# First mixer: scores from a stacked 128-row product and one of 64 rows, merge factors from one product of 48 rows

## What is computed

```python
for g, (win, dil) in enumerate(DILATED_GROUPS):
    o, lse = dilated_band_attention(q[:, :, g], k[:, :, g], v[:, :, g], win, dil)
    # inside: s = einsum('nbqhd,nbphd->nhbqp', q_blocks, key_band) / sqrt(64); softmax; times v
y = merge_by_denominator(outs, lses)      # softmax over the 3 groups' lse, weighted sum
y = y @ w_o
```

## Time and profile before

| | us |
|---|---|
| median of 3 runs | 3315.78 (3310.75 to 3321.85) |
| the profiled execution's own time | 3310.81 |
| its span in the profile | 3309.0 |
| PE busy | 3141.3 (95%) |
| PE weight loads busy | 3039.6 (92%) |
| VectorE, ScalarE, GpSimd busy | 1784.8, 1620.8, 1700.9 |
| mean granted TensorE clock | 0.974 of full |

### The profile page before, as it was taken

The page is one execution under the profiler, slowest core; times in us unless marked ns, Lnnn a source line. Parts: engine busy times, 40 slices in busy tenths (PEclk is TensorE's granted clock), DMA queues, the critical chain, the costliest instruction groups (busy, mean ns, idle before and its releaser), DMA issues. The chain is left out here.

```text
span 3309.0 us, 56628 instructions
## 1 busy us (share of the span) xinstructions
PE 3141.3 (95%) x21560; PEld 3039.6 (92%) x21560; DVE 1784.8 (54%) x3643; ACT 1620.8 (49%) x3402; POOL 1700.9 (51%) x1420
## 2 busy tenths in 40 slices
PE   8999999999999968999999999689889999999997
PEld 7999999999999948999999999688878999999997
DVE  4445445454554537765463465348867653533653
ACT  4555555555555514454353354247745543543542
POOL 5555555555555505665465465343336654554663
PEclk9999999999999979999999999799989999999998
DMA  5666666676667275333444444211153344444443
GB/s 202 244 241 218 231 234 224 215 258 217 234 229 257 87 273 188 128 134 126 139 137 134 147 137 147 90 48 40 46 176 120 130 135 134 156 136 141 162 144 98
DMA packets 134861, 540.74 MB, mean 163 GB/s; under 512 B 25008, under 2 KB 49376, under 8 KB 131760
## 3 DMA queue, kind: packets, MB, share of 16 engines
q1 hardware_dynamic: 133392, 535.79, 47.8%
q10 hardware_dynamic: 784, 1.12, 0.1%
q0 software_dynamic: 416, 0.21, 0.0%
HBM read 497.34 MB, written 216.90 MB: 216 GB/s over the span
## 5 line engine op out<-in xcount | busy, mean ns | idle before, releaser
L1236 ACT CAST t_w_hi<-t_raw 128x1024 fp32r<-128x1024 f32 (+1 forms) x456 | 468.2, 1027 | 796.0 <-PE t_bank L103 732.0
L101 PE MATMUL t_bank<-x_hi,t_w_hi 128*128 128x352 f32 (+1 forms) x2112 | 680.9, 322 | 6.0 <-DVE x_lo L1530 2.7
L102 PE MATMUL t_bank<-x_lo,t_w_hi 128*128 128x352 f32 (+1 forms) x2112 | 675.1, 320 | 0.0
L1359 POOL TENSOR_TENSOR t_w_lo<-t_raw,t_w_hi 128x1024 fp32r<-128x1024 f32 (+1 forms) x228 | 544.4, 2388 | 253.1 <-ACT t_w_hi L1236 253.1
L103 PE MATMUL t_bank<-x_hi,t_w_lo 128*128 128x352 f32 (+1 forms) x2112 | 671.9, 318 | 0.0
L1437 DVE TENSOR_TENSOR t_w_lo<-t_raw,t_w_hi 128x1024 fp32r<-128x1024 f32 (+1 forms) x228 | 326.7, 1433 | 639.9 <-ACT t_w_hi L1236 639.9
L101 PE MATMUL a_gemm<-x_hi,a_w_hi 128*128 128x352 f32 (+1 forms) x1728 | 564.0, 326 | 11.3 <-DVE x_lo L620 11.3
L102 PE MATMUL a_gemm<-x_lo,a_w_hi 128*128 128x352 f32 (+1 forms) x1728 | 553.8, 321 | 0.0
L103 PE MATMUL a_gemm<-x_hi,a_w_lo 128*128 128x352 f32 (+1 forms) x1728 | 551.8, 319 | 0.0
L101 PE MATMUL t_bank<-t_h_hi,t_w_hi 128*128 128x352 f32 (+1 forms) x1440 | 466.6, 324 | 33.0 <-DVE t_h_lo L1443 24.9
L103 PE MATMUL t_bank<-t_h_hi,t_w_lo 128*128 128x352 f32 (+1 forms) x1440 | 463.3, 322 | 0.0
(11 more groups left out here) (280 smaller groups left out, 5799.6 us busy)
## 6 DMA issues: line engine op xcount, KB each, us to landing
t_raw<-w_up SPq DMA_DIRECT2D x264, 512.0 KB, 3.7
roll<-cache SPq DMA_DIRECT2D x128, 1023.5 KB
t_raw<-w_down SPq DMA_DIRECT2D x96, 512.0 KB, 3.6
a_raw<-w_a SPq DMA_DIRECT2D x72, 512.0 KB, 4.5
roll<-cache SPq DMA_DIRECT2D x16, 2044.0 KB
t_raw<-w_o SPq DMA_DIRECT2D x48, 512.0 KB, 3.6
t_raw<-w_down SPq DMA_DIRECT2D x48, 384.0 KB, 3.1
vT<-a_vt SPq DMA_DIRECT2D x24, 516.0 KB, 6.7
```

Of the source, the lines that this page charges most:

```text
L101: pe.matmul(out, w_hi, x_hi, start=first, stop=False)
L102: pe.matmul(out, w_hi, x_lo, start=False, stop=False)
L1236: act.copy(w_hi[:, b % RING, cols], raw[:, b % RING, cols]).then_inc(s_whi, 1)
L1359: pool.tensor_tensor(w_lo[:, b % RING, cols], raw[:, b % RING, cols], f32(w_hi[:, b % RING, cols]), ALU.subtract).then_inc(s_wlo[0], 1)
```

## The change

Three edits, all in `mixer_a`:

- **Scores.** The keys' high part and low part of a head stand under one another in one tile `k_both` (own 64 partitions: high; the other 64: low), and the queries' high part stands twice (`q_twice`). One matmul of 128 rows makes q_hi·k_hi + q_hi·k_lo; one of 64 rows adds q_lo·k_hi. Per query block the order is: 128 rows head 0, 128 rows head 1, 64 rows head 0, 64 rows head 1.
- **The parts' making.** ACT writes the high part in two copies of 64 partitions (one a head), and for queries in two more to the other half; POOL subtracts in two instructions of 64 partitions. POOL's next turn also waits until its own last subtraction is done, and from `s_qtwo` that the copies of the queries have read `qp`; PE's `scores` at s = 0 wait for `s_qtwo` too.
- **Factors.** High and low factors stand in one tile `f_both` of 48 rows (0 to 15 and 32 to 47, zeros between), and `sel` holds its matrix twice, so that one matmul of 48 rows takes the place of two of 16. The merge weighs in place, and two additions take the place of the reduction.

```diff
@@ scalar: high_turned
-                act.copy(class_tiles(kq_hi[i1 % 2][:, r // 3, :], g1)[:, :, a:b],
-                         class_major(qp[:, r % 2, 0:n], g1)).then_inc(s_kqhi, 1)
+                dst = (k_both, q_twice)[r // 3][i1 % 2]
+                for h in range(2):
+                    last = act.copy(class_tiles(dst[own_half(h), h, :], g1)[:, :, a:b],
+                                    class_major(qp[own_half(h), r % 2, 0:n], g1))
+                last.then_inc(s_kqhi, 1)
+                if r >= 3:
+                    for h in range(2):
+                        last = act.copy(class_tiles(dst[other_half(h), h, :], g1)[:, :, a:b],
+                                        class_major(qp[own_half(h), r % 2, 0:n], g1))
+                    last.then_inc(s_qtwo, 1)
@@ gpsimd: turn
+                need(pool, s_qtwo, 3 * i1 + (-1, 0, 0, 0, 0, 1)[r])
...
-                pool.tensor_tensor(lo, class_major(qp[:, r % 2, 0:n], g1), f32(hi), ALU.subtract).then_inc(s_kqlo, 1)
+                hi_of = (k_both, q_twice)[r // 3][i1 % 2]
+                for h in range(2):
+                    lo = k_both[i1 % 2][other_half(h), h, :] if r < 3 else q_lo[i1 % 2][own_half(h), :]
+                    last = pool.tensor_tensor(class_tiles(lo, g1)[:, :, a:b],
+                                              class_major(qp[own_half(h), r % 2, 0:n], g1),
+                                              f32(class_tiles(hi_of[own_half(h), h, :], g1)[:, :, a:b]), ALU.subtract)
+                last.then_inc(s_kqlo, 1)
+                need(pool, s_kqlo, k + 1)
@@ vector: merge_tile
-                dve.tensor_reduce(o[:, p % 2, 0, j * P:(j + 1) * P], fbm[:, :, :].rearrange("p g t -> p t g"),
-                                  op=ALU.add, axis=AX_X).then_inc(s_fbr, 1)
+                dve.tensor_tensor(weighed[:, 0, :], weighed[:, 0, :], weighed[:, 1, :], ALU.add).then_inc(s_fadd, 1)
+                need(dve, s_fadd, k + 1)
+                dve.tensor_tensor(weighed[:, 0, :], weighed[:, 0, :], weighed[:, 2, :], ALU.add).then_inc(s_fbr, 1)
@@ tensor: spread_factors and scores
-                pe.matmul(x_bank[:, 0:NG * P], sel[:, j, :], rhs[0], start=True, stop=False)
-                pe.matmul(x_bank[:, 0:NG * P], sel[:, j, :], rhs[1], start=False, stop=True).then_inc(s_fb, 1)
+                pe.matmul(x_bank[:, 0:NG * P], sel[:, j, :], f_both[:, :, :].rearrange("r g t -> r (g t)"), start=True,
+                          stop=True).then_inc(s_fb, 1)
...
                     for h in range(2):
-                        rows = slice(HD * h, HD * h + HD)
...
-                        product(pe, s_bank[h][:, 2 * P * j + w0:2 * P * (j + 1)],
-                                kq_hi[i % 2][rows, 1, q_cols], kq_lo[i % 2][rows, 1, q_cols],
-                                kq_hi[i % 2][rows, 0, k_cols], kq_lo[i % 2][rows, 0, k_cols],
-                                True, True).then_inc(s_scores, 1)
+                        pe.matmul(out[h], q_twice[i % 2][:, h, q_cols], k_both[i % 2][:, h, k_cols], start=True, stop=False)
+                    for h in range(2):
+                        rows = own_half(h)
+                        pe.matmul(out[h], q_lo[i % 2][rows, q_cols], k_both[i % 2][rows, h, k_cols], start=False,
+                                  stop=True).then_inc(s_scores, 1)
```

More of the change, by code:

```diff
@@ L191, in mixer_a, with small_rows @@
         o = sb("o", [P, 2, NG, T])
-        fbm = sb("fbm", [P, NG, P])
         st = sb("st", [P, 2, 96])
         stT = sb("stT", [96, P])
[L195 to L199, removed]
-        qs, ks = (sb(name, [P, NG, PAIRS, NS]) for name in ("qs", "ks"))
[L201 to L205, removed]
+        qs, ks = (sb(name, [P, NG, PAIRS, NS]) for name in ("qs", "ks"))
+        with ExitStack() as upper:
+            f_both, sel = (upper.enter_context(nc.sbuf_tensor("a_" + name, shape, F32R)) for name, shape in (
+                ("f_both", [48, NG, P]), ("sel", [48, QT, P])))
+        f_hi, f_lo = f_both[0:16], f_both[32:48]
+        below = sb("below", [P, (2 * NG + QT) * P])
+        def small_rows(first, n, shape):
+            return below[64:80, first * P:(first + n) * P].rearrange(shape, g=NG, t=P)
+        sr = small_rows(0, 2 * NG, "r (w g t) -> r w g t")
+        dd, mw = (small_rows(k * NG, NG, "r (g t) -> r g t") for k in (2, 3))
+        mt = below[64:80, 4 * NG * P:(4 * NG + 1) * P]
+        fw = below[0:16, (NG + QT) * P:(2 * NG + QT) * P].rearrange("r (g t) -> r g t", g=NG)
+        q_lo = [sb(f"q_lo{i}", [P, SEQ], F32R) for i in range(2)]
+        k_both, q_twice = [None, sb("k_both1", [P, 2, SEQ], F32R)], [None, sb("q_twice1", [P, 2, SEQ], F32R)]
         with ExitStack() as lent:
@@ L213, in mixer_a @@
             w_lo = sb_lent("w_lo", [P, 2, KT, P])
-            kq_hi[0] = sb_lent("kq_hi0", [P, 2, SEQ])
-            kq_lo[0] = sb_lent("kq_lo0", [P, 2, SEQ])
+            k_both[0] = sb_lent("k_both0", [P, 2, SEQ])
+            q_twice[0] = sb_lent("q_twice0", [P, 2, SEQ])
         units_kv = sb("units_kv", [P, 8, KT, P])
@@ L227, in mixer_a @@
         s_whi, s_wlo, s_gemm, s_evac = (sem(x) for x in ("whi", "wlo", "gemm", "evac"))
-        s_shuf, s_t1, s_t2, s_qp, s_kqhi, s_kqlo = (sem(x) for x in ("shuf", "t1", "t2", "qp", "kqhi", "kqlo"))
+        s_shuf, s_t1, s_t2, s_qp, s_kqhi, s_kqlo, s_qtwo, s_fadd = (
+            sem(x) for x in ("shuf", "t1", "t2", "qp", "kqhi", "kqlo", "qtwo", "fadd"))
         kq_out = [sem("kq_out0"), sem("kq_out1")]
@@ L292, in stats_due, with own_half, other_half @@
             return q if 0 <= i < NI and q > 0 and g == 0 and s == 2 else None
+        def own_half(h):
+            return slice(HD * h, HD * h + HD)
+        def other_half(h):
+            return own_half(1 - h)
         def first_key(u, j):
@@ L498, in evacuate @@
                     if i1 == 0:
-                        act.wait_ge(s_sel, 1)
+                        act.wait_ge(s_sel, 2)
                 need(act, s_gemm, 9 * i1 + c + 1)
@@ L622, in _ @@
             dve.wait_ge(s_const, 16 * 6)
-            dve.tensor_copy(sel[:, :, :].rearrange("r j f -> r (j f)"), vt[0:16, 0:QT * P]).then_inc(s_sel, 1)
+            dve.tensor_copy(f_both[0:32, :, :].rearrange("r g t -> r (g t)"), vt[0:32, 0:NG * P]).then_inc(s_sel, 1)
+            dve.wait_ge(s_sel, 1)
+            dve.tensor_copy(sel[:, :, :].rearrange("r j f -> r (j f)"), vt[0:48, 0:QT * P]).then_inc(s_sel, 1)
             def natural(ap3, g):
@@ L833, in scores @@
                     need(pe, s_kqlo, 6 * (i + 1))
+                    need(pe, s_qtwo, 3 * (i + 1))
                 if u == 0:
@@ L838, in scores @@
                     t, w0 = 2 * s + j, first_key(u, j)
+                    q_cols, k_cols = slice(t * P, (t + 1) * P), slice((t - 1) * P + w0, (t + 1) * P)
+                    out = [s_bank[h][:, 2 * P * j + w0:2 * P * (j + 1)] for h in range(2)]
                     for h in range(2):
-                        rows = slice(HD * h, HD * h + HD)
-                        q_cols, k_cols = slice(t * P, (t + 1) * P), slice((t - 1) * P + w0, (t + 1) * P)
-                        product(pe, s_bank[h][:, 2 * P * j + w0:2 * P * (j + 1)],
-                                kq_hi[i % 2][rows, 1, q_cols], kq_lo[i % 2][rows, 1, q_cols],
-                                kq_hi[i % 2][rows, 0, k_cols], kq_lo[i % 2][rows, 0, k_cols],
-                                True, True).then_inc(s_scores, 1)
+                        pe.matmul(out[h], q_twice[i % 2][:, h, q_cols], k_both[i % 2][:, h, k_cols], start=True, stop=False)
[3 more added lines that the diff above has]
+                                  stop=True).then_inc(s_scores, 1)
             def weigh_values(u):
@@ L2370, in shape_constants @@
         mask_c=np.where((q <= i) & (q // HD == i // HD), f(0), big).astype(f))
-    sel = np.zeros((2 * QT, QT, P), f)
+    sel = np.zeros((48, QT, P), f)
     for r in range(2 * QT):
-        sel[r, r % QT, HD * (r // QT):HD * (r // QT) + HD] = 1
-    out["sel"] = sel.reshape(2 * QT, QT * P)
+        for part in (0, 32):
+            sel[part + r, r % QT, HD * (r // QT):HD * (r // QT) + HD] = 1
+    out["sel"] = sel.reshape(48, QT * P)
     row = np.arange(P)
```

10 lines of the change are left out of this document (4 added, 6 removed).

## The result

| us | before | after |
|---|---|---|
| median (4 runs each) | 3313.27 (3308.93 to 3321.85) | 3465.43 (3461.82 to 3469.63) |
| the profiled execution's own time | 3310.81 | 3461.82 |
| mean granted TensorE clock | 0.974 | 0.960 |

The changed kernel takes 1.0456 times as long (95% interval 1.0432 to 1.0480). I had predicted 3400 us and a range of 3330 to 3432: the direction is right, the size is not, and the time lies outside the range.

The account below looks back on a forecast made before the run. PE was taken to bound the loop, busy 1081.9 of 1083.0 us. Own time 3310.8 + 24.7 (PE's own sum) + 64.8 (waits for POOL) = 3400.3 us; forecast 3400 us, range 3330 to 3432.

Parts of the forecast that it names:

- Slots on PE: Scores on PE: three slots a block as before, 64-row pairs sharing one, narrow 128-row products at 0.115 us; no time saved.
- Changes of height: PE switching between matmuls of different row counts: 0.14 us (narrow) or 0.19 us (wide) each, 31.3 + 4.5 us in all.
- The spread: Factors' spread on PE: the low part's product goes, 0.18 us x 56 = -10.1 us in the loop.
- POOL's and ACT's chain: Making of key and query parts: each POOL turn +1.9 us from ACT's two copies and POOL's two subtractions.
- PE's waits for the scores: PE waiting for POOL: 8 x 4.5 us (group 1) + 8 x 3.1 us (group 2) + some 4 us (first set).
- ACT's evacuations of chunks 6 to 8: Projection chunks on PE waiting for ACT's evacuations, held back by turn 4's copies: counted at nothing.
- The wait in group 0: PE before group 0's scores: POOL done at 619.1 against PE at 620.0, so no wait, but only just.
- rival C: Sixteen PE waits of some 4 us lower the clock, losing 2 us more each: 3432 us; chance 0.10.
- my own walk: Group-1 set followed turn by turn on the earlier trace's clock: POOL done at 670.8, PE ready at 666.3, waiting 4.5 us.
- Rival A: Only the changes between row counts on PE cost; POOL's halves are cheap or slack suffices: 3336 us; chance 0.15.
- B: Not slower: the gaps read as row-count changes on PE belong to semaphore waits, new order free: 3291 us; chance 0.07.

Follow-up runs that it names:

- the run grouped by height: Kernel before, with each unit's scores as four products of 128 rows, then four of 64 rows: 3321.03 us, ratio 1.0018.
- The last filled run: Changed kernel, with 20, 11 and 9 filler matmuls of 512 columns ahead of group 1's scores, group 2's scores and the waiting spread: 3432.52 us, ratio 1.0362.
- the runs on height: Kernel before, with only the scores reordered: 128, 64, 128, 64 rows, 3347.75 us; all 128-row products first, then 64-row ones, 3321.03 us.

## Why the prediction was right, and where it failed

**Slots on PE: right.** Each block has three slots, the pairs of 64 rows stand as x2, and the narrow products of 128 rows take the 0.115 us that I put for them (0.48 us for four in the run grouped by height). A unit of two narrow blocks, after:

```profile
666.68 0.33 PE L874 MATMUL a_scores<-a_k_both,a_q_twice 128*128 128x128 f32 x2
666.94 0.33 PE L877 MATMUL a_scores<-a_k_both,a_q_lo 64*128 64x128 f32 x2
667.20 0.44 PE L874 MATMUL a_scores<-a_k_both,a_q_twice 128*128 128x128 f32 x2
667.57 0.33 PE L877 MATMUL a_scores<-a_k_both,a_q_lo 64*128 64x128 f32 x2
667.83 0.39 PE L101 MATMUL a_pv<-a_pt_hi,a_v_hi 128*128 128x256 f32 x1
```

**Changes of height: right in size, wrong in the sum.** 31.3 + 4.5 us were predicted, 32 to 35 measured by themselves. But I added them to the waits, and in sets that POOL's chain decides they cost next to nothing (the run with scores in 64 rows: 5 us, not clear of nothing).

**The spread: right,** 10.0 us of 10.1 in the loop. That it would wait (7 times, at most 1.9 us) I had not seen. It stands in front of a wait for POOL which would only be longer without it, so I take it to cost by the clock at most; no run shows it by itself.

**POOL's and ACT's chain: right for groups 0 and 1, a little short for group 2.** From turn 1 to the last subtraction I had +3.8, +8.3 (662.49 to 670.8) and +7.3 us; measured are +3.79, +8.31 and +8.28. A half costs as much as a whole on POOL, as I chose. PE's waits for the scores came to 71.0 us for the 64.8 of the prediction, and those for ACT's evacuations of chunks 6 to 8, which I put at nothing, to 1.7. The wait in group 0, put at nothing too, is nothing (0.05), but the slack I left it is gone.

**The clock: the step that failed.** It stood in the text as rival C, at 2 us for each of sixteen waits, with a chance of 0.10, so that my forecast held none of it. In fact the records show a low stretch with nearly every wait for scores (17 in the loop and at its end, most of them 6.8 us long, beginning 1 to 2 us before the wait is over), and it makes the next first piece 2.2 to 2.5 us longer, on the path: PE must reach the chunk that POOL turns before POOL's chain can begin. The last filled run shows it: the low clock is gone but for 10 us, these pieces are back within 0.7 us of before, and POOL's chain is as it was. The condition was in my own walk (waits of 3 to 5 us, sixteen times) and the earlier trace rows showed the level. The trace of before had the evidence too, and I had not read it: PE's longest wait in the earlier trace rows, 2.4 us, ends at 53.73, and the stretch behind it reads

```profile
54.00:60.00 6.00, 6.00 (x37) 5.78 (x36) 1.89 (x9) 2.76 (x10) 2.37 (x1) 0.73 0.70 219
```

PE busy throughout, the granted clock 0.73. The one wait of this length in front of scores was followed by the lower clock. That is a single case, but it speaks against a chance of 0.10.

The sum again, for three sets, by the medians of the table: the chain +3.79 + 8.31 + 8.28 = +20.4; the slack given up -3.66 - 2.60 - 3.19 = -9.5; PE's first piece at full clock (the filled run) +0.65 + 0.63 + 0.68 = +2.0; the low clock +2.51 + 0.05 + 2.22 = +4.8. Together 17.7, eight times 142 us; the loop grew by 150, the rest lies in the first sets and in means above medians. The prediction had 24.7 + 64.8 = 89.5. What is missing there: the clock, 8 x 4.8 = 38 us; group 2's chain, 8 x 1.0 = 8 us; some 10 us by which PE's work and the waits, which do not simply add, came to more than I put for them; and 5 in the first sets. The last two of these terms are worked out as a remainder, and no run shows them apart. With the clock in the sum the prediction would have been 3438 us, still 27 below the 3465 measured; and the last filled run, with 10 us at the lower clock left in the loop, takes 3432.5 and not 3400. So the clock is the largest part of the miss, 38 of 61 us by the pieces (31 by the filled run), and not all of it.

Rival A (heights only) falls with the waits, B with the runs on height. C had the mechanism; its 3432 us had too little for each stretch (2.0 for 2.4; it took the low clock to last some 4 us behind a wait, and it lasts some 5.5) and, like the forecast, for group 2.

## What to carry to other kernels

When a change takes the slack of a chain beside PE, count the sets in which PE will wait, and add for each the low clock behind the wait as part of the likeliest case, not as a mishap. Do not add PE's own extra work to waits: in a set that another engine decides, only what lies between PE's release and that engine's next start counts. Group matmuls by their number of rows; and before splitting an instruction over partitions on GpSimd or ScalarE, expect each half to cost what the whole did.

## What the runs showed of the hardware that I had not expected

- Half the partitions save nothing. On POOL the subtraction has a mean of 1.06 to 1.09 us for 64 partitions by 352, and had 1.075 for 128 partitions by 352. On ACT the means of the copy of the same two shapes are 0.71 and 0.715 us. POOL before, then after:

```profile
L579 POOL TENSOR_TENSOR a_kq_lo<-a_qp,a_kq_hi 128x352 fp32r<-128x352 f32 x96 | 103.2, 1075 | 121.2 <-ACT a_kq_hi L488 121.2
L603 POOL TENSOR_TENSOR a_q_lo<-a_qp,a_q_twice 64x352 fp32r<-64x352 f32 x96 | 104.8, 1092 | 80.6 <-ACT a_q_twice L504 77.8
L603 POOL TENSOR_TENSOR a_k_both<-a_qp,a_k_both 64x352 fp32r<-64x352 f32 x96 | 101.7, 1059 | 105.1 <-ACT a_k_both L504 102.3
```

- A kernel can be made faster by giving a waiting engine useless work: the fill took 31 us off, with no piece of the chain shortened but those at the lower clock. The Trainium skill (TensorE: Matmul & The Clock Gate, Terms) reckons half of the time at the lower level as lost. By that 119.5 us would cost 60; this case shows 31 (the filled run) to 38 (the pieces). One reason is in the trace: 22 of the 119.5 us fall into waits, where PE has nothing to do. The rest of the difference is not told apart.
- Not every difference in rows costs in full. In the run of the spread alone, one matmul of the scores' first pair (64 rows) starts 0.01 us behind a spread of 48 rows and the other 0.28 us behind it, where both stood 0.27 us behind the 16-row one in the earlier trace rows. Likely the early one is head 1's, whose 64 partitions the spread doesn't use; the rows do not name the head. A projection matmul of 128 rows starts 0.37 us behind the spread of 48 rows.

```profile
605.32 0.44 PE L828 MATMUL a_vT_factors<-a_f_both,a_sel 48*128 48x384 f32 x1
605.33 0.32 PE L101 MATMUL a_scores<-a_kq_hi 64*128 64x128 f32 x1
...
605.60 0.22 PE L101 MATMUL a_scores<-a_kq_hi 64*128 64x128 f32 x1
```
